# A two-block transformer kernel: two first weight streams on x without the token factor, row-wise loads of small tensors

## What is computed

```python
def rms_norm(x, g):
    xf = x.astype(jnp.float32)
    y = xf * lax.rsqrt(jnp.mean(xf * xf, axis=-1, keepdims=True) + EPS)
    return (y * g.astype(jnp.float32)).astype(x.dtype)

def compress(kv, pe, w1, w2):
    ...
    blocks = blocks + pe[None, None, :, None, :]
    hid = jax.nn.silu(jnp.einsum('bnlgd,lde->bnge', blocks, w1))
    return jnp.einsum('bnge,ef->bngf', hid, w2)

h = rms_norm(x, norm_g[l])
proj = h @ w_in[l]
q, kv, g_logits, z_a, uv, z_b, merge_logits = jnp.split(proj, SPLIT_IDX, axis=-1)
```

## Time and profile before

| | us |
|---|---|
| median of 3 runs | 2220.66 |
| lowest, highest | 2220.34, 2220.76 |
| the profiled execution | 2222.62 |
| its span, first to last instruction | 2220.9 |
| PE busy | 2189.9 |

### The profile page before, as it was taken

How to read it: one execution, slowest core, us unless ns; L and a number is a source line. 1 busy time by engine, 2 the same in 40 slices (tenths; PEclk the granted TensorE clock), 3 DMA queues, 4 the chain that set the end, 5 groups by cost and what they waited for, 6 DMA issues and landing times.

```text
span 2220.9 us, 42710 instructions
## 1 busy us (share of the span) xinstructions
PE 2189.9 (99%) x18291; PEld 2150.6 (97%) x18291; DVE 1506.7 (68%) x2603; ACT 1087.4 (49%) x1603; POOL 418.5 (19%) x349
## 2 busy tenths in 40 slices
PE   7999999999999999999999999999999999999998
PEld 7999999999999999999999999999999999999998
DVE  5555666664565567668999988769856447777564
ACT  4345555544544455354334666554535454444443
POOL 5110000000000000088788400470001001110000
PEclk9999999999999999999999999999999999999999
DMA  7865445656566655555555556566655555555662
GB/s 221 196 120 186 152 153 173 193 157 193 182 190 190 185 179 170 171 180 172 167 175 173 168 175 174 170 189 179 188 171 172 175 164 170 171 162 152 206 189 95
DMA packets 378791, 385.86 MB, mean 174 GB/s; under 512 B 14086, under 2 KB 371862, under 8 KB 378408
## 3 DMA queue, kind: packets, MB, share of 16 engines
q1 hardware_dynamic: 374394, 378.54, 56.0%
q0 software_dynamic: 2464, 3.21, 1.6%
q10 hardware_dynamic: 1744, 1.38, 0.2%
HBM read 380.72 MB, written 4.12 MB: 173 GB/s over the span
## 4 chain that ended last, share of the span: by engine, by line
PE 88%; DVE 7%; DMA 2%; ACT 1%; issue 1%; SPq 1%; POOL 0%; ACTq 0%; DVEq 0%
PE ps L480 27%; PE ps L490 27%; PE ps L485 27%; DMA raw<-in_w_in_dram 2%; DVE ps L1899 2%; DVE wlo L431 1%; PE ps L2676 1%; PE ps L2725 1%; ACT whi L424 1%; PE ps L2521 1%; PE ps L2492 0%; PE ps L2504 0%; PE ps L2745 0%; DVE op_lo L562 0%; DVE arena L2021 0%
## 5 line engine op out<-in xcount | busy, mean ns | idle before, releaser
L424 ACT ACTIVATE whi<-raw 128x1024 fp32r<-128x1024 f32 (+1 forms) x688 | 724.3, 1057 | 885.4 <-PE ps L490 849.9
L431 DVE TENSOR_TENSOR wlo<-raw,whi 128x1024 fp32r<-128x1024 f32 x550 | 670.3, 1228 | 461.8 <-ACT whi L424 460.7
L480 PE MATMUL ps<-op_hi,whi 128*128 128x256 f32 (+1 forms) x5440 | 786.4, 287 | 5.7 <-DVE op_lo L1450 4.2
L485 PE MATMUL ps<-op_lo,whi 128*128 128x256 f32 (+1 forms) x5440 | 772.6, 284 | 1.1 <-DVE op_lo L1766 0.6
L490 PE MATMUL ps<-op_hi,wlo 128*128 128x256 f32 (+1 forms) x5440 | 771.7, 284 | 0.4 <-POOL wlo L431 0.3
L480 PEld LDWEIGHTS ps<-op_hi,whi 128*128 128x128 f32 x5440 | 705.5, 188 | 15.4 <-issue 6.6
L485 PEld LDWEIGHTS ps<-op_lo,whi 128*128 128x128 f32 x5440 | 706.5, 188 | 1.7 <-DVE op_lo L1766 0.8
L490 PEld LDWEIGHTS ps<-op_hi,wlo 128*128 128x128 f32 x5440 | 705.8, 188 | 0.9 <-POOL wlo L431 0.5
L431 POOL TENSOR_TENSOR wlo<-raw,whi 128x1024 fp32r<-128x1024 f32 x134 | 324.0, 2421 | 1044.7 <-ACT whi L424 1044.3
L1899 DVE SCALAR_TENSOR_TENSOR ps<-arena,param_cols,ps 128x257 f32<-128x257 f32 (+6 forms) x448 | 183.4, 492 | 0.4
L1581 DVE SCALAR_TENSOR_TENSOR arena<-arena,nslopes,ps 128x128 f32<-128x128 f32 (+1 forms) x64 | 23.5, 410 | 47.7 <-PE ps L2492 46.2
(11 more groups left out here) (396 smaller groups left out, 1352.3 us busy)
## 6 DMA issues: line engine op xcount, KB each, us to landing
raw<-in_e_w_in_dram SPq DMA_DIRECT2D x96, 1024.0 KB, 5.4
raw<-in_w_in_dram SPq DMA_DIRECT2D x84, 1024.0 KB, 5.2
raw<-in_o_w_in_dram SPq DMA_DIRECT2D x64, 1024.0 KB, 5.7
raw<-in_e_w_out_dram SPq DMA_DIRECT2D x32, 1024.0 KB, 5.3
raw<-in_w_out_dram SPq DMA_DIRECT2D x16, 1024.0 KB, 5.3
raw<-in_w_ple_gate_dram SPq DMA_DIRECT2D x16, 1024.0 KB, 5.3
raw<-in_o_w_out_dram SPq DMA_DIRECT2D x16, 1024.0 KB, 5.4
arena<-cum_rows SPq DMA_DIRECT2D x16, 544.0 KB, 6.3
```

The lines of the kernel that those rows point to most:

```text
L424: nc.scalar.activation(hi_view(c, n), half_view(raw[c % RING], c, n), ACT.Copy).then_inc(hi_ready, 1)
L431: own.tensor_tensor(lo_view(c, n), half_view(raw[c % RING], c, n), hi_view(c, n).bitcast(F), ALU.subtract).then_inc(lo_sem[kind], 1)
L480: nc.tensor.matmul(o, hi8[c % 2][:, k, n * P:(n + 1) * P], MH[:, t, off:off + NT], start=(i % cpp == 0 and k == 0 and not (joint and n)), ...
L485: nc.tensor.matmul(o, hi8[c % 2][:, k, n * P:(n + 1) * P], ML[:, t, off:off + NT], start=False, stop=False, skip_group_check=joint)
```

## The change

1. "kvc" and "qa" are multiplied with x times the gain, without the token's factor (`multiply_x`). ACT makes op_hi tile by tile from the turned x in PSUM (`x_split_hi`), DVE op_lo (`x_split_lo`); ACT splits chunks 0 and 1 of the weights in between. The factor is applied when DVE evacuates the two streams (`x_evac`), so these evacuations move from ACT to DVE.
2. Squares of the second half of x, root, diagonal and `rstd` come later; PE spreads the factors after chunk 2. The normalized operand h1 is built while "qa" runs (`h1_scale`, `h1_hi`, `h1_lo`, buffers H1) and is used from "qb" on.
3. x is loaded half by half rather than token tile by token tile; there are five filling matmuls.
4. The parameter rows are loaded from ACT's queue after the last squares, and the load of 31 rows is cut into 16 and 15. `raw_x` comes after "qa".
5. Positions are loaded as rows (`pe_rows`, 4 DMAs of 32 rows) and turned by PE (`turn_pe`) and copied by DVE; POOL issues them after "kvc". The skip weights come in one DMA as rows on all partitions (`d_rows`), and two DVE copies pick the columns.
6. blocks(0) moves behind the first chunk of "qb", hidden(0) behind its third, the key product and hidden(1) behind its fourth.

```diff
-FILL = 4
+FILL = 5
+        H1 = [ar(at, 4, S1) for at in (1024, 3072, 4096, 8640)]
+        X_BANK = (0, 4, 2, 6)
+        X_PARTS = [(tt, half) for half in range(2) for tt in range(2)]
...
-            load_stream(sp_eng, "kvc", between=load_params)
-            for n in ("qa", "qb", "kvs"):
+            for n in ("kvc", "qa", "qb", "kvs"):
...
-                    for b in range(2):
-                        nc.gpsimd.dma_start(peT[o, j, b], A[f"cmp_pe_{nm}"][0].rearrange("(l b) d -> b d l", b=2)[b],
-                                            allow_slow_non_contiguous=True).then_inc(landed, 16)
...
+            pool.wait_ge(half_done, 2 * ST["kvc"].end)
+            for j in range(2):
+                for half in range(2):
+                    nc.gpsimd.dma_start(pe_rows[0:CMP_LEN, j, HD * half:HD * half + HD], A[f"cmp_pe_{'kv'[j]}"][0]).then_inc(S("pe_landed"), 16)
...
-            for half in range(2):
-                src = bass.AP(A["e_D_2"].tensor, half, [[0, HD], [2, DT]])
-                nc.gpsimd.dma_start(Dcol[HD * half:HD * (half + 1), :], src, allow_slow_non_contiguous=True).then_inc(S("d_landed"), 16)
+            nc.gpsimd.dma_start(d_rows[:, :], bass.AP(A["e_D_2"].tensor, 0, [[0, P], [1, 2 * DT]])).then_inc(S("d_landed"), 16)
...
+            def x_split_hi(g_):
+                act.wait_ge(S("h1_psum"), g_ + 2)
+                for t in range(4 * g_, 4 * g_ + 4):
+                    nc.scalar.activation(MH[:, t, 0:S1], x_psum(g_)[:, t % 4, :], ACT.Copy, scale=GC[:, t:t + 1]).then_inc(S("xh_ready"), 1)
+
+            x_square(0)
+            x_square(1)
+            act.wait_ge(S("x_diag"), 1)
+            x_split_hi(0)
+            x_split_hi(1)
             split_hi(act, 0, 0)
+            x_split_hi(2)
+            split_hi(act, 0, 1)
+            x_split_hi(3)
+            split_hi(act, 1, 0)
+            split_hi(act, 1, 1)
+            x_square(2)
+            x_square(3)
...
+                         (A["e_dw_w_2"][0][0:16], R_DW, 16),
+                         (A["e_dw_w_2"][0][16:K31], R_DW + 16, K31 - 16),
...
+                for src, r, n in srcs:
+                    nc.scalar.dma_start(PR[r:r + n, :], src).then_inc(S("params_landed"), 16)
...
+            side("kvc", extra=x_root)
+            side("qa", pre=h1_early)
+            h1_hi(2)
+            h1_hi(3)
...
+            x_split_lo(0)
+            raw_copy(0)
+            x_split_lo(1)
+            x_split_lo(2)
+            x_split_lo(3)
+            raw_copy(1)
+            raw_copy(2)
+            raw_copy(3)
...
+            side("kvc", x_evac(8, 1.0), extra=h1_first)
+            side("qa", x_evac(0, HD ** -0.5), pre=h1_rest, extra=raw_x)
+            h1_lo(2)
+            h1_lo(3)
             side("qb", extra=value_blocks)
...
+            for c in range(ST["qa"].end):
+                for n in range(2):
+                    multiply_x(c, n)
+                if c == 2:
+                    rstd_rows()
+            raw_x(3)
+            stream_pe(pe, "qb", need="h1", hi=1)
+            turn_pe()
+            stream_pe(pe, "qb", need="h1", lo=1, hi=3)
             hidden(0)
-            stream_pe(pe, "qb", lo=1, hi=2)
+            stream_pe(pe, "qb", lo=3)
```

More of the change, by code:

```diff
@@ L1475, in _ @@
[L1475 to L1487 removed]
+                V.tensor_tensor(op(ML, S1)(g_), H1[g_], op(MH, S1)(g_).bitcast(F), ALU.subtract).then_inc(ml_ready, 1)
@@ new lines, in _, with x_evac, evac @@
+            dve.wait_ge(S("factor_rt"), 2)
+            v.do(V.reciprocal(ms[:, 8:10], ms[:, 6:8]))
+            v.sync()
+            for tt in range(2):
+                V.tensor_scalar(DG[:, tt], ident[:, :], ms[:, 8 + tt:9 + tt], None, ALU.mult).then_inc(S("x_diag"), 1)
+            dve.wait_ge(S("h1_psum"), 6)
+            V.tensor_copy(rstd[:, 0:S1], ps[:, 6, 0:S1]).then_inc(S("x_diag"), 1)
+            dve.wait_ge(S("x_diag"), 4)
+            dve.wait_ge(S("xT_copied"), 4)
+            def x_evac(base, scale):
+                def evac(j, par):
+                    V.scalar_tensor_tensor(out=qkvT[:, base + 2 * j:base + 2 * j + 2, :], in0=ps[:, pairof(par), 0:S1], scalar=scale,
+                                           in1=rstd[:, 0:S1].unsqueeze(1).to_broadcast([P, 2, S1]), op0=ALU.mult, op1=ALU.mult) \
+                        .then_inc(acc_free, 1)
+                return evac
@@ L1987, in _ @@
             dve.sem_inc(S("tri_free"), 1)
+            dve.wait_ge(S("d_landed"), 16)
+            for half in range(2):
+                o = slice(HD * half, HD * half + HD)
+                v.do(V.tensor_copy(Dcol[o, :], d_rows[o, :].rearrange("p (t h) -> p t h", h=2)[:, :, half]))
+            v.sync()
             side("bc", conv5("bc", 1), extra=conv_tile(8))
@@ L2373, in _ @@
             pe.wait_ge(S("norm_g_landed"), 16)
-            T.transpose(ps[:, 7, S1:S1 + DT], NGR[0:DT, :], ident[0:DT, 0:DT]).then_inc(S("h1_psum"), 1)
+            T.transpose(ps[:, 7, 0:DT], NGR[0:DT, :], ident[0:DT, 0:DT]).then_inc(S("h1_psum"), 1)
             def x_turn(t, tt):
-                return T.transpose(h1_psum(t // 4)[:, t % 4, P * tt:P * tt + P], xnat[:, tt, t * P:t * P + P], ident[:, :])
-            for part in range(4):
+                return T.transpose(x_psum(t // 4)[:, t % 4, P * tt:P * tt + P], xnat[:, tt, t * P:t * P + P], ident[:, :])
@@ L2380, in _ @@
+            for part, (tt, half) in enumerate(X_PARTS):
                 pe.wait_ge(S(f"x_landed_{part}"), 16)
-                for t in range(8 * (part % 2), 8 * (part % 2) + 8):
-                    if part >= 2 and t % 4 == 0 and t < 12:
-                        pe.wait_ge(S("xT_copied"), t // 4 + 1)
-                    if (part, t) == (1, 14):
-                        pe.wait_ge(S("x_diag"), 1)
-                    if t < DT - 1:
-                        mm = x_turn(t, part // 2)
-                    if t % 4 == 3:
+                if part == 2:
+                    pe.wait_ge(S("x_diag"), 1)
+                for t in range(8 * half, 8 if half == 0 else 12):
+                    mm = x_turn(t, tt)
+                    if tt == 1 and t % 4 == 3:
@@ L2389, in _ @@
                         mm.then_inc(S("h1_psum"), 1)
-            for tt in range(2):
-                pe.wait_ge(S("x_diag"), tt + 2)
-                T.matmul(ps[:, 7, S1 + P * tt:S1 + P * tt + P], ones[:, :], DG[:, tt], start=True, stop=True).then_inc(S("h1_psum"), 1)
-            pe.wait_ge(S("x_diag"), 4)
             for i in range(FILL):
                 T.matmul(ps[:, 7, S1:2 * S1], ident[:, :], xnat[:, 0, S1 * i:S1 * i + S1], start=True, stop=True)
-            for tt in range(2):
-                mm = x_turn(DT - 1, tt)
+            for t in range(12, DT):
+                for tt in range(2):
+                    mm = x_turn(t, tt)
@@ L2407, in raw_x, with turn_pe @@
                         mm.then_inc(S("pc_psum"), 1)
+            def turn_pe():
+                pe.wait_ge(S("pe_landed"), 64)
+                pe.wait_ge(S("pc_ready"), 4)
+                for j in range(2):
+                    mm = T.transpose(ps[:, 5, CMP_LEN * j:CMP_LEN * (j + 1)], pe_rows[0:CMP_LEN, j, :], ident[0:CMP_LEN, 0:CMP_LEN])
+                mm.then_inc(S("pe_psum"), 1)
             def hidden(j):
```

224 lines of the change are left out of this document (118 added, 106 removed).

## The result

| | before | after |
|---|---|---|
| median, us | 2220.71 (4 runs) | 2209.03 (4 runs) |
| lowest, highest | 2220.34, 2220.90 | 2208.73, 2209.11 |
| the profiled execution | 2222.62 | 2209.04 |
| its span | 2220.9 | 2207.0 |

The ratio is 0.9945, with a 95% interval of 0.9933 to 0.9957: faster by 11.7 us, clear of noise. The forecast was 2206.7 us with a range of 2203.7 to 2213.0. The time lies in the range, 2.3 us above the forecast. As a ratio the forecast is 0.9937, which lies inside the interval, so the 2.3 us are not clear of noise by themselves. The price of rival 1, 2209.8 us, is nearer to the measured time than the forecast is; only the traces tell the two apart.

A forecast was written before the change was run, and what follows sets the result against it. PE bounds the kernel, busy 2189.9 of 2220.9 us. Terms 4.5 + 5.4 - 0.6 + 4.6 - 0.2 = 13.7, plus 0.3 for handoffs, 14.0 us: profiled 2208.6, median 2206.7 us, range 2203.7 to 2213.

The forecast's parts named there:

- rival 1: Near 19 us the clock falls all the same, for as long as before: 3.1 us, 2209.8 us; chance 0.06.
- Start of the stream: First weight stream: normalization leaves the path, so PE starts at 13.9 us instead of 18.42, 4.5 us gained.
- Inside the first chunks: Chunks of "kvc": three old waits and the low clock go, 0.5 us of new wait comes, 5.4 us gained.
- own sign of 88.3 us: First "kvs" chunk, which began at 98.18 us before, was to begin near 88.3 us.
- ACT's row issues at nothing: ACT's 14 row DMA issues, ahead of chunk 2's split, run beside its other work and cost nothing.
- rival 2: ACT's row issues hold the split of chunk 2: 1.5 to 3.3 us or more, 2208 to 2213 us; chance 0.09.
- Skip weights, 4.6 us: Near 172 us: one broadcast replaces 2048 elements, removing a 2.85 us PE wait and 1.7 us of low clock.
- DVE's thin cover: h1's third low group, ready at 65.9 us, wanted at 66.8: cover 0.9 us, up to 1 us at risk, 0.1 taken.
- the two terms for the low clock: Time lost at the lower clock level: 3.1 us in the first chunks, 1.7 us behind the wait at 172.35 us.
- The third: Rows keep one DMA engine busy ahead of chunks, so chunk 2 is late: 11.7 us, 2218.4 us; chance 0.05.
- The fourth: The wait near 172 us stays, as POOL's 16 small copies use the same queue: 2211.3 us; chance 0.06.
- The fifth: Slower: ACT's DMA issues block its own splits, PE waits 23.5 us: 2233 us; chance 0.02.

The follow-up runs named there:

- e11: Changed kernel with chunk 0 loaded between the quarters of x and the turns of tiles 8 to 15 behind the first products: 2208.49 us, ratio 0.9940.
- e5: Changed kernel with the 31 parameter rows in one load again, still on ACT's queue: 2215.52 us, ratio 0.9972.
- e3: Kernel before, with only the skip weights loaded as broadcast rows plus two DVE copies: 2218.03 us, ratio 0.9982.
- e4: Changed kernel with the skip weights loaded as single elements again: 2211.24 us, ratio 0.9956.
- e1: Kernel before, unchanged, run and profiled once more: 2221.85 us, ratio 1.0002.
- e2: Kernel before, with only the 31-row load cut into 16 and 15, still on SP's queue: 2218.23 us, ratio 0.9986.
- e10: Changed kernel with the positions loaded element by element again, without PE's turn and the copy: 2209.86 us, ratio 0.9945.
- e12: Changed kernel, unchanged, run again on another chip: 2209.44 us, ratio 0.9943.

## Why the prediction held, and where it was off

**Start of the stream.** Forecast 13.9 us, measured 14.11: right, 0.2 us short. Two prices in the walk were off and nearly harmless. ACT's tile of x took 0.38 us (3.03 us for 8), not the 0.27 read off a quarter of a wide activation, and the last part of x held the turns a little longer. e11 shows where the tile price does bind.

**Inside the first chunks.** The wait for the first wlo half is 0.33 us (forecast 0.5). From 14.11 to 31.70 us PE does 18 groups in 17.6 us, where 18 x 0.94 is 16.9. Nothing waits for chunk 2. At "kvs" the lead is 9.1 us; the terms up to there give 9.6, and the prediction's own sign of 88.3 us (9.9) had left out two of them.

**ACT's row issues at nothing.** Right, shown by the rows of ACTq beside ACT; rival 2 did not come. Why the first issue on SP took 3.79 us, a full queue as the prediction has it or another cause, no row shows. Their bytes were the danger, not their issue, and only while they lay on one engine (e5).

**Skip weights, 4.6 us.** The lead grew from 8.9 us (159.04 against 150.12 us at L2585) to 13.4 us at L2597: 4.5 us in this pair of executions. By the ratios it is 4.0 us in the kernel before (e3) and 2.4 in the changed one (e4). The wait was sized right; its low clock lasted 3.4 us in one execution, 6.9 us in e1 and was absent from e2.

**DVE's thin cover** for h1's third low group held: PE shows no wait near 66 us. e10 shows what it costs when a chunk is late: 1.1 us.

**Sum.** 14.0 us forecast for the profiled execution, 13.9 us measured in the span. Of the profiled executions, 2208.6 us was forecast and 2209.04 measured. So close an agreement is in part luck. Behind the second place, where all terms are in, the lead is 13.4 us; the last 0.5 us came later, where the forecast has no term, and the 0.3 us added for handoffs show nowhere.

**The step that failed** is the last one: "The profiled execution took 2222.62 us, 1.96 us over the median of 2220.66 us; it would become 2208.6 us, the median 2206.7 us". I carried the 1.96 us over as if it were a property of the profiler. In the changed kernel there is no such difference: 2209.04 us profiled against a median of 2209.03, and 2209.26 against 2209.44 in e12. In the kernel before, the profiled execution was one of the long ones. It had 10.2 us at the low clock, and by e1 the low stretch at either place can be 3.4 us shorter, which is 1.7 us of time. What lies outside the span adds 0.3 us. So the two terms for the low clock, 3.1 and 1.7 us, were sized by an execution of that kind and are most likely too large for the median by about 1.7 us together. That is worked out, not seen: both profiles of before are long executions, and none of a usual one was taken. Nor is the shortfall itself beyond noise. The median fell by 11.7 us here and by 12.2 us on the chip of e12.

**Rivals.** None came. The windows at 1.00 rule out the first. The third was real, kept away by the cut: undone, it costs 6.5 us on ACT's queue and, with the old place, 11.5 us. I had given the cut no term of its own, though of the edits that were tried alone none takes more away. The fourth (the second place stays) was wrong: no wait there. The fifth's blocking issues of 13 us on ACT did not occur; the longest row issue on ACTq took 0.51 us.

## What to carry to other kernels

A median and a profiled execution differ by what varies in the kernel. Before their difference is carried over to a forecast, ask whether the change removes the very stretch that varies; here the low-clock time behind waits of 2 to 3 us was most likely such a stretch. Two edits that free the same engine from two different waits are not a sum: an earlier start was worth about -3.6 us with a late chunk behind it and +5.8 us without. The load of 31 rows, a number without a large divisor, was cheap to cut into 16 and 15. Such a load is worth cutting before anything is moved earlier. And count the chunks before a cover is read off: I took the split of chunk 3 for that of chunk 4 and read a cover of some 7 us, where the first has about 1 and the second about 4.
